# Squares of two norms added up on GpSimd and summed once by TensorE; the last norm's weights applied by feature and its turns moved ahead of the last products

## The chip, the cores and the metric

The kernel runs on one core of a Trainium2 chip. The core has TensorE (PE in the profile, with its weight loads as PEld), VectorE (DVE), ScalarE (ACT), GpSimd (POOL) and SyncE (SP), and 16 DMA engines that all queues share. The metric is the time of one execution on the device in microseconds; less is better.

## What is computed

One layer of a decoder, for a prompt of 512 tokens and for 8 sequences of 4 new tokens each (the sample group) that read a paged cache of keys and values. All is float32, the model is 1024 wide.

```python
h = _rmsnorm(x, norm1_w) * (1 + sc1) + sh1
z = h @ w_in                                  # 8 retention heads, 8 block-attention heads
...
x = x + g1 * (jnp.concatenate([ret_out, moba_out], axis=-1) @ w_out)
h2 = _rmsnorm(x, norm2_w) * (1 + sc2) + sh2   # the second norm
x = x + g2 * ((jax.nn.silu(h2 @ w_gate) * (h2 @ w_up)) @ w_down)
...
y_prompt = _rmsnorm(xp, final_w)              # the last norm
y_sample = _rmsnorm(xs, final_w)

def _rmsnorm(x, w):
    y = x * lax.rsqrt(jnp.mean(x * x, axis=-1, keepdims=True) + NORM_EPS)
    return y * w
```

## The kernel before

Everything is placed by hand: each engine has its own written-out order of instructions, and semaphores (`wait_ge`, `then_inc`) join them. No scheduler moves anything. Prompt activations lie turned, features on the 128 partitions and the 512 tokens along the row, so a tile `x2T[:, k, :]` (128x512) is feature tile k of eight (KT = 8). Products are made in three matmuls (`L1128` high part by high part, `L1129` low part of the activation, `L1130` low part of the weight).

Beside the prompt's work runs the sample group's attention over the cache, cut into 64 slots (page groups of 4 pages of 128 rows). In slot s, GpSimd has gathered the keys of the group into one of two buffers (`gather(g)`, L523, 1 MB, asynchronous; gather g waits until VectorE has turned group g - 2), VectorE turns them (L1846), TensorE multiplies them with the queries (`keys(s)`, L1161, at the slot's head), and 12 slots later TensorE weighs the values (`weigh`, L1216), whose pages SyncE loads as their buffers come free. At slots that are a multiple of 8, VectorE makes the block sums (L1859 to L1862) right behind the turn of the next group, and TensorE takes them (`block_gates`, L1180).

The output projection is slots 43 to 50 (`R_OUT` = 43, f = 0 to 7), one tile f of 24 matmuls in each. VectorE adds tile f to the residual (`residual`, L2126), and ScalarE squares it into one of two buffers (`stage[f % 2]`, L950). TensorE then sums each square over its features: `sum_squares(k)`, four 128x1 matmuls against ones (eight records in the trace, L1551), adding all eight tiles up in a PSUM bank. After the eighth, VectorE, ScalarE, TensorE and GpSimd turn the sums into 1/rms for each token, spread over all partitions in `rb`, and scale and split the tiles (slots 51 to 53) before the FFN's first product.

In GpSimd's order stand, beside the gathers, the rotation of the sample's queries and keys in iterations 46 and 47 (L532 to L535, products with `pool.drain()` between them; the next instruction does not start before the drain is done), two masked products in iteration 48 (L541), and the eight scalings of the norm in iterations 54 and 55 (L566).

The down projection, `R_DOWN`, is 24 steps d, 6 for each pair of feature tiles; steps 4 and 5 of a pair finish its two tiles, `evict_down` adds them to the residual. The last norm of the prompt comes after all of them: TensorE turns the eight feature tiles back into four token tiles of 128x1024 (32 turns of 128x128, L1722), ScalarE squares each with a running sum (L1058) and takes the root (L1060), VectorE inverts (L2332) and multiplies with 1/rms and with the weights `fw`, which lie along the row (L2334), and SyncE stores the tile (L512):

```python
for i in range(TT):
    final_norm(i)      # VectorE: wait for root i, reciprocal, scale by 1/rms and fw
```

The vectors that are needed by feature (norm weights among them) are loaded as rows at the start into `vrow`, by five small loads on ScalarE's queue, and turned by TensorE into `vT`, one column for each feature tile.

## Time and profile before

| | |
|---|---|
| median of 3 runs | 1039.37 us (1035.85 to 1046.96) |
| profiled execution, its own time | 1034.07 us |
| its span in the trace | 1032.2 us |
| mean granted clock of TensorE | 0.976 |
| busy: PE, DVE, ACT, POOL | 961.6, 624.5, 338.4, 139.4 us |
| DMA moved | 269.14 MB, 261 GB/s on the mean |

The span runs from the first to the last record; the profiled execution took 1.9 us more around it. Busy times are sums of records and say nothing of who waits for whom; the chain of waits does, from the last instruction back to the first.

### The profile page before, as it was taken

How to read it: one execution, taken by the hardware profiler on the slowest of the kernel's cores; microseconds unless marked ns; L12 is line 12 of the kernel's file. 1: busy time of each engine (PE TensorE's matmuls, PEld its weight loads, DVE VectorE, ACT ScalarE, POOL GpSimd, SP SyncE). 2: the span in 40 equal slices, each digit the busy share in tenths (PEclk: the TensorE clock that was granted, in tenths of full speed). 3: DMA queues.
4: the chain of work that ended last, by engine and by line, in shares of the span. 5: the costliest groups of instructions: out<-in, count | busy, mean ns of one | idle time of the engine just before them, and what ended most of it. 6: DMA issues, size and time to landing. Idle time of an engine off the chain costs nothing.

```text
span 1032.2 us, 20974 instructions
## 1 busy us (share of the span) xinstructions
PE 961.6 (93%) x7919; PEld 675.8 (65%) x7919; DVE 624.5 (60%) x1067; ACT 338.4 (33%) x735; POOL 139.4 (14%) x129
## 2 busy tenths in 40 slices
PE   3879998999999987979989999999999999999996
PEld 2557775766666644547756767676777777777775
DVE  1566874677767667876788584432655555453244
ACT  5412233334333624542252152332333222121113
POOL 0011111444210132204151220000000000000000
PEclk9899999999999989999989899999999999999998
DMA  9978877999786889988998668778476988787652
GB/s 340 364 257 282 284 252 268 296 274 300 255 287 215 276 320 390 356 288 280 362 320 285 231 230 265 230 228 267 144 218 167 240 226 231 218 251 248 204 194 87
DMA packets 217973, 269.14 MB, mean 261 GB/s; under 512 B 13473, under 2 KB 168425, under 8 KB 209682
## 3 DMA queue, kind: packets, MB, share of 16 engines
q1 hardware_dynamic: 110226, 126.65, 38.7%
q10 hardware_dynamic: 98432, 74.04, 23.6%
q0 software_dynamic: 9216, 67.11, 17.7%
q8 instruction: 63, 1.03, 0.4%
q14 instruction: 36, 0.29, 0.1%
HBM read 260.04 MB, written 5.64 MB: 257 GB/s over the span
## 4 chain that ended last, share of the span: by engine, by line
PE 72%; DVE 8%; DMA 7%; issue 5%; SPq 4%; DVEq 2%; ACT 1%; POOLq 1%; POOL 1%; ACTq 0%
PE banks L1128 13%; PE banks L1129 12%; PE banks L1130 12%; PE banks L1078 6%; PE banks L1216 4%; PE banks L1141 4%; PE banks L1143 4%; PE banks L1142 4%; PE banks L1161 4%; DVE KT L1846 3%; DMA V<-in_cache_v 3%; DMA K<-in_cache_k,kidx 1%; SPq L420 1%; PE banks L1340 1%; DMA early<-in_w_mod 1%
## 5 line engine op out<-in xcount | busy, mean ns | idle before, releaser
L658 ACT ACTIVATE whi<-raw 128x1024 fp32r<-128x1024 f32 (+1 forms) x76 | 78.6, 1035 | 298.0 <-PE banks L1130 144.4
L1128 PE MATMUL banks<-ahi,whi 128*128 128x512 f32 x416 | 169.2, 407 | 0.1
L1846 DVE STREAM_TRANSPOSE KT<-K 128x2048 f32<-128x2048 f32 x63 | 145.5, 2310 | 30.0 <-DMA K<-in_cache_k,kidx 15.1
L1129 PE MATMUL banks<-alo,whi 128*128 128x512 f32 x416 | 163.5, 393 | 0.0
L1130 PE MATMUL banks<-ahi,rawlo 128*128 128x512 f32 x416 | 163.3, 393 | 0.0
L1809 DVE TENSOR_TENSOR rawlo<-raw,whi 128x1024 fp32r<-128x1024 f32 (+1 forms) x76 | 91.3, 1201 | 54.3 <-ACT whi L658 51.2
L523 POOL DMA_INDIRECT K<-in_cache_k,kidx x64 | 64.0, 1000 | 412.4 <-DVE KT L1846 363.7
L1128 PEld LDWEIGHTS banks<-ahi,whi 128*128 128x128 f32 x416 | 78.7, 189 | 31.2 <-issue 13.1
L1141 PE MATMUL banks<-ahi,whi 128*128 128x512 f32 x216 | 90.2, 417 | 1.2 <-DVE rawlo L1816 0.9
L1130 PEld LDWEIGHTS banks<-ahi,rawlo 128*128 128x128 f32 x416 | 78.8, 189 | 17.3
L1161 PE MATMUL banks<-KT,qbd 128*32 128x128 f32 x2048 | 74.0, 283 | 15.7 <-DVE KT L1846 13.0
L1129 PEld LDWEIGHTS banks<-alo,whi 128*128 128x128 f32 x416 | 78.8, 189 | 14.9
L1143 PE MATMUL banks<-ahi,rawlo 128*128 128x512 f32 x216 | 85.1, 394 | 0.0
L1142 PE MATMUL banks<-alo,whi 128*128 128x512 f32 x216 | 84.9, 393 | 0.0
L1161 PEld LDWEIGHTS banks<-KT,qbd 128*32 128x32 f32 x2048 | 56.7, 112 | 29.7 <-issue 14.1
L1216 PE MATMUL banks<-V,pT 128*32 128x512 f32 x368 | 64.4, 630 | 11.5 <-DMA V<-in_cache_v 11.4
L1816 DVE TENSOR_TENSOR rawlo<-raw,whi 128x1024 fp32r<-128x1024 f32 x28 | 35.8, 1279 | 30.4 <-ACT whi L651 14.9
L1141 PEld LDWEIGHTS banks<-ahi,whi 128*128 128x128 f32 x216 | 40.9, 190 | 17.9 <-issue 7.5
L748 ACT ACTIVATE pm<-banks,st 128x128 f32<-128x128 f32 (+3 forms) x32 | 16.6, 524 | 96.8 <-DVE st L1989 91.4
L1143 PEld LDWEIGHTS banks<-ahi,rawlo 128*128 128x128 f32 x216 | 40.8, 189 | 9.4
L1142 PEld LDWEIGHTS banks<-alo,whi 128*128 128x128 f32 x216 | 41.1, 190 | 7.3
L1750 DVE TENSOR_TENSOR xtmp<-xtmp,banks 32x256 f32<-32x256 f32 x90 | 37.5, 417 | 7.1 <-issue 0.4
(330 smaller groups left out, 1462.1 us busy)
## 6 DMA issues: line engine op xcount, KB each, us to landing
V<-in_cache_v SPq DMA_DIRECT2D x184, 256.0 KB
rawm<-in_w_mod ACTq DMA_DIRECT2D x14, 1024.0 KB
raw<-in_w_in ACTq DMA_DIRECT2D x12, 1024.0 KB
zT<-in_cache_v SPq DMA_DIRECT2D x48, 256.0 KB
raw<-in_w_gate ACTq DMA_DIRECT2D x22, 512.0 KB
raw<-in_w_up ACTq DMA_DIRECT2D x22, 512.0 KB
srw<-in_w_gate SPq DMA_DIRECT2D x22, 512.0 KB, 5.6
srw<-in_w_up SPq DMA_DIRECT2D x22, 512.0 KB, 7.3
```

What stands on the lines that cost most here:

```text
L523: pool.indirect_dma_start(Kb[g % 2][:, :], None, ck, bass.IndirectOffsetOnAxis(kidx[:, g:g + 1], 0)).then_inc(s_k[g % 2], 16)
L658: act.activation(whi[t % 2][:, 0:kd, :], raw[u][:, 0:kd, t % 2 * P:(t % 2 + 1) * P], ACT.Copy).then_inc(s_hi, 1)
L1128: pe.matmul(out[:, :], whi[t % 2][:, k, :], hi(k), start=(first and n == 0), stop=False)
L1129: pe.matmul(out[:, :], whi[t % 2][:, k, :], lo(k), start=False, stop=False)
L1130: last = pe.matmul(out[:, :], low[:, k, :], hi(k), start=False, stop=(final and n == kd - 1))
L1141: pe.matmul(DB[:, :], whi[m % 2][:, k, :], ahi[:, k, :], start=(k == 0), stop=False)
L1142: pe.matmul(DB[:, :], whi[m % 2][:, k, :], alo[:, k, :], start=False, stop=False)
L1143: last = pe.matmul(DB[:, :], wlow[:, k, :], ahi[:, k, :], start=False, stop=(k == KT - 1))
L1161: last = pe.matmul(LG[32 * gq:32 * gq + 32, (g % 4) * P:(g % 4 + 1) * P], qbd[g // NGRP % 2][:, j, :], KTb[:, :, j, :], start=(jj == 0), s ...
L1216: pe.matmul(VO[32 * pg:32 * pg + 32, :], pT[:, n, 32 * pg:32 * pg + 32], bufs[pg][:, :], start=(n == 0), stop=(n == NGRP - 1)).then_inc(s_ ...
L1809: tt(rawlo[u][:, 0:kd, cols], raw[u][:, 0:kd, cols], whi[t % 2][:, 0:kd, :].bitcast(F32), ALU.subtract).then_inc(s_lo, 1)
L1846: dve.transpose(KTb[:, :, :, :], Kb[g % 2][:, :]).then_inc(s_kt, 1)
```

## The change

For the second norm, ScalarE squares feature tile 0 into `rb`, and tiles 1 to 6 into the two stage buffers as before. GpSimd adds tile k (1 to 6) into `rb` in iteration 47 + k of its loop (`add_squares`), between a gather and the next, and drains before it counts up `s_sqa`. ScalarE waits for that count instead of TensorE's before it uses a stage buffer again. TensorE makes two groups of sums, one of `rb` and one of tile 7, both after the last tile.

For the last norm the same is done in buffers `x3q(k)`: ScalarE squares each tile after its eviction, GpSimd adds tiles 1 to 6 into tile 0, and TensorE sums twice. VectorE multiplies each evicted tile by its weights (`vT`, eight more columns, from a sixth small load on ScalarE's queue) into `x3w(k)`, and TensorE turns these instead of `x2T`: 18 turns (three token tiles, features 0 to 5) go ahead of the last two product tiles, the other 14 stay behind. One inverse and one root serve all four token tiles; ScalarE scales tiles 0 and 2 out of PSUM and VectorE tiles 1 and 3. The sample group's last norm is as it was.

```diff
--- before.py
+++ after.py
@@ -40,8 +40,8 @@
 NMOD, NMA = 24, 8
-V_BMOD, V_N1, V_N2, V_GN, V_MN = 0, 48, 56, 64, 68
-NVEC = 72
+V_BMOD, V_N1, V_N2, V_GN, V_MN, V_FW = 0, 48, 56, 64, 68, 72
+NVEC = 80
@@ -276,6 +276,10 @@
     fw = at(A, "fw", [P, DM])
     ytok = [at(A + 1024 + DM * i, f"ytok{i}", [P, DM]) for i in range(TT)]
+    x3q = lambda k: ytok[k // 2][:, k % 2 * T:(k % 2 + 1) * T]
+    xwb = at(A + 1024 + DM * TT, "xwb", [P, KT - 2, T])
+    x3w = lambda k: xwb[:, k, :] if k < KT - 2 else stage[k - KT + 2]
     two_banks = [persist.enter_context(nc.psum_tensor(f"banks{i}", [P, 2, 512], F32)) for i in range(4)]
     bank01 = two_banks[0]
     bank = [two_banks[i // 2][:, i % 2, :] for i in range(8)]
@@ -352,7 +356,7 @@
+    s_nx, s_gmt, s_sqa = sem("x2_scaled"), sem("gmod_turned"), sem("x2_squares_added")
...
+    X3Q, X3A, X3W, X3S, X3I, X3R = KT, KT - 2, KT, 2, RSPREAD, 1
     kview = lambda w: w[0].rearrange("(k p) f -> p k f", p=P)
     w_mod_v, w_in_v, w_out_v = kview(w_mod), kview(w_in), kview(w_out)
@@ -508,7 +516,7 @@
         sp.wait_ge(s_y, 1)
         sp.dma_start(y_sample.rearrange("b t d -> (b t) d"), x2s[:, :]).then_inc(s_out, 16)
         for i in range(TT):
-            sp.wait_ge(s_y, i + 2)
+            sp.wait_ge((s_yr, s_y)[i % 2], i // 2 + 2)
             sp.dma_start(y_prompt[0, i * P:(i + 1) * P, :], ytok[i][:, :]).then_inc(s_out, 16)
         sp.wait_ge(s_kss, 48)
         sp.wait_ge(s_kst, 64)
@@ -565,10 +573,20 @@
                 pool.wait_ge(s_r1, RSPREAD)
             pool.tensor_tensor(zT[:, k, :], zT[:, k, :], rb[:, :], ALU.mult).then_inc(s_nx, 1)
+        def add_squares(k):
+            pool.wait_ge(s_sqx, k + 1)
+            pool.tensor_tensor(rb[:, :], rb[:, :], stage[k % 2][:, :], ALU.add)
+            pool.drain().then_inc(s_sqa, 1)
         def scale_heads(hp):
             pool.wait_ge(s_hrs, hp + 2)
             o = rettok[:, hp, :].rearrange("p (c d) -> p c d", d=HD)
             pool.tensor_tensor(o, o, gain[:, hp, 0:8].unsqueeze(2).broadcast_to((P, H, HD)), ALU.mult).then_inc(s_hn, 1)
+        def add_x3_squares(k):
+            pool.wait_ge(s_sqx, X3Q + k + 1)
+            pool.tensor_tensor(x3q(0), x3q(0), x3q(k), ALU.add)
+            pool.drain().then_inc(s_sqa, 1)
         pool.wait_ge(s_idx, 1)
         pool.wait_ge(s_hi, 1)
@@ -589,6 +607,8 @@
                 pool.wait_ge(s_hrs, 1)
                 heads = mobatok.rearrange("p i (h d) -> p i h d", h=H)
                 pool.tensor_tensor(heads, heads, gain[:, 4:8, 0:8].unsqueeze(3).broadcast_to((P, TT, H, HD)), ALU.mult).then_inc(s_hm, 1)
+            if 1 <= g - R_OUT - 4 < KT - 1:
+                add_squares(g - R_OUT - 4)
             if g in (R_NORM + 3, R_NORM + 4):
                 for k in range(4):
                     scale_x(4 * (g - R_NORM - 3) + k)
@@ -614,12 +634,16 @@
                 masked_k(b)
                 masked_k(b + 1)
+        for k in range(1, KT - 1):
+            add_x3_squares(k)
     @block.scalar
     def _(act):
         act.dma_start(vrow[V_BMOD:V_N1, :], b_mod[0].rearrange("(r c) -> r c", c=P)).then_inc(s_vec, 16)
         for a, v in ((V_N1, norm1_w), (V_N2, norm2_w), (V_GN, ret_gn_w), (V_MN, moba_norm_w)):
             n = v.shape[1] // P
             act.dma_start(vrow[a:a + n, :], v[0].rearrange("(r c) -> r c", c=P)).then_inc(s_vec, 16)
+        act.dma_start(vrow[V_FW:NVEC, :], final_w.rearrange("(r c) -> r c", c=P)).then_inc(s_vec, 16)
         act.dma_start(xs[:, :], x_sample.rearrange("b t d -> (b t) d")).then_inc(s_xs, 16)
         act.wait_ge(s_c, 32)
         act.activation(crow[:, :], crow[:, :], ACT.Silu).then_inc(s_silu, 1)
@@ -945,9 +969,9 @@
                 split_out(f + 1)
             if f >= 1:
                 act.wait_ge(s_ev, F_OUT + f + 2)
-                if f >= 3:
-                    act.wait_ge(s_ssm, f - 2)
-                act.activation(stage[(f - 1) % 2][:, :], x2T[:, f - 1, :], ACT.Square).then_inc(s_sqx, 1)
+                if f >= 4:
+                    act.wait_ge(s_sqa, f - 3)
+                act.activation(rb[:, :] if f == 1 else stage[(f - 1) % 2][:, :], x2T[:, f - 1, :], ACT.Square).then_inc(s_sqx, 1)
             if f == KT - 1:
                 exps(B_NORM)
             if f:
@@ -957,7 +981,7 @@
         act.activation(st2[:, 28:29], C("eps"), ACT.Sqrt)
         act.wait_ge(s_ev, F_OUT + KT + 2)
-        act.wait_ge(s_ssm, KT - 2)
+        act.wait_ge(s_sqa, KT - 3)
         act.activation(stage[1][:, :], x2T[:, KT - 1, :], ACT.Square).then_inc(s_sqx, 1)
         slot(R_NORM)
         next_chunk(5)
@@ -1043,6 +1067,10 @@
                 keep_gate(m // 2)
             sample_slot(s)
             slot(s)
+        def x3_squares(k):
+            act.wait_ge(s_ev, F_DOWN + k + 1 + 2)
+            act.activation(x3q(k), x2T[:, k, :], ACT.Square).then_inc(s_sqx, 1)
         for d in range(6 * DM // CHUNK):
             t = KT + 2 * FT + d
             if d % 2 == 0:
@@ -1052,12 +1080,19 @@
             if d == 0:
                 keep_hidden(FT - 1)
             sample_slot(R_DOWN + d)
-        for i in range(TT):
-            act.wait_ge(s_yt, i + 1)
-            act.activation(ytok[i][:, :].rearrange("p (e c) -> p e c", e=2), TURNED[i][:, :, :], ACT.Square, accum_out=st[:, 16 + i:17 + i])
-            act.drain()
-            act.activation(st2[:, 16 + i:17 + i], st[:, 16 + i:17 + i], ACT.Sqrt, scale=1.0 / DM, bias=C("eps")).then_inc(s_yr, 1)
+            fb, e = divmod(d - 5, 6)
+            if fb >= 0 and e < 2:
+                x3_squares(2 * fb + e)
+        x3_squares(KT - 1)
+        act.wait_ge(s_r1, X3I + 1)
+        act.activation(st2[:, 24:28], st2[:, 16:20], ACT.Sqrt).then_inc(s_r2, 1)
+        act.drain()
+        for i in (0, 2):
+            act.wait_ge(s_yt, 1)
+            act.activation(ytok[i][:, :].rearrange("p (e c) -> p e c", e=2), TURNED[i][:, :, :], ACT.Copy,
+                           scale=st2[:, 24 + i:25 + i]).then_inc(s_yr, 1)
     @block.tensor
     def _(pe):
@@ -1067,7 +1102,7 @@
         for k in range(KT):
             last = pe.transpose(bank[4][:, k * NSEQ:(k + 1) * NSEQ], crow[:, k * P:(k + 1) * P], ident[0:NSEQ, 0:NSEQ])
         last.then_inc(s_ctp, 1)
-        pe.wait_ge(s_vec, 80)
+        pe.wait_ge(s_vec, 96)
         pe.transpose(bank[5][:, 0:NVEC], vrow[:, :], ident[0:NVEC, 0:NVEC]).then_inc(s_vtp, 1)
         pe.wait_ge(s_ct, 1)
@@ -1543,14 +1578,18 @@
-        def sum_squares(k):
-            if k == 0:
-                pe.matmul(DB[:, 0:TT], ident, C("pad0")[:, 0:TT], start=True, stop=False, skip_group_check=True)
-            pe.wait_ge(s_sqx, k + 1)
+        def sum_over_features(out, src, final):
             for i in range(TT):
-                last = pe.matmul(DB[:, i:i + 1], stage[k % 2][:, i * P:(i + 1) * P], ones[:, 0:1], start=False, stop=(k == KT - 1),
-                                 skip_group_check=True)
-            last.then_inc(s_ssm, 1)
+                last = pe.matmul(out[:, i:i + 1], src[:, i * P:(i + 1) * P], ones[:, 0:1], start=False, stop=final, skip_group_check=True)
+            return last
+        def sum_squares():
+            pe.matmul(DB[:, 0:TT], ident, C("pad0")[:, 0:TT], start=True, stop=False, skip_group_check=True)
+            pe.wait_ge(s_sqa, KT - 2)
+            sum_over_features(DB, rb, False)
+            pe.wait_ge(s_sqx, KT)
+            sum_over_features(DB, stage[1], True).then_inc(s_ssm, 1)
         for f in range(KT):
             slot_head(R_OUT + f)
@@ -1564,11 +1603,9 @@
                  last_in=(lambda: turn_heads(3)) if f == 0 else None)
             if f == KT - 1:
                 slot_head(R_NORM)
-            if f:
-                sum_squares(f - 1)
             if f == KT - 1:
                 turn_probs(B_NORM, 0)
-                sum_squares(KT - 1)
+                sum_squares()
             slot_rest(R_OUT + f)
@@ -1704,6 +1741,9 @@
             sample_slot(s)
             slot_rest(s)
+        def turn_x3(i, k):
+            return pe.transpose(TURNED[i][:, k // 4, (k % 4) * P:(k % 4 + 1) * P], x3w(k)[:, i * P:(i + 1) * P], ident)
         for d in range(6 * DM // CHUNK):
             fb, n, half = d // 6, d // 2 % 3, d % 2
             pe.wait_ge(s_fl, 8 * n + KD[n] + 1)
@@ -1712,15 +1752,33 @@
             tile(KT + 2 * FT + d, bank[2 * (fb % 2) + half], lambda k: unit(8 * n + k)[:, 0], lambda k: unit(8 * n + k)[:, 1],
                  KD[n], first=(n == 0), final=(n == 2))
             sample_slot(R_DOWN + d)
-        for i in range(TT):
-            for k in range(KT):
-                if i == 0 and k == 0:
-                    pe.wait_ge(s_ev, F_DOWN + 7 + 2)
-                if i == 0 and k == KT - 1:
-                    pe.wait_ge(s_ev, F_DOWN + 8 + 2)
-                last = pe.transpose(TURNED[i][:, k // 4, (k % 4) * P:(k % 4 + 1) * P], x2T[:, k, i * P:(i + 1) * P], ident)
-            last.then_inc(s_yt, 1)
+            if d == 6 * DM // CHUNK - 3:
+                pe.wait_ge(s_x3, 1)
+                pe.wait_ge(s_nx, X3W + KT - 2)
+                for i in range(TT - 1):
+                    for k in range(KT - 2):
+                        turn_x3(i, k)
+        pe.wait_ge(s_nx, X3W + KT - 1)
+        for i in range(TT - 1):
+            turn_x3(i, KT - 2)
+        for k in range(4):
+            turn_x3(TT - 1, k)
+        pe.wait_ge(s_nx, X3W + KT)
+        for i in range(TT - 1):
+            last = turn_x3(i, KT - 1)
+        last.then_inc(s_yt, 1)
+        sums = TURNED[TT - 1][:, 1, :]
+        pe.matmul(sums[:, 0:TT], ident, C("pad0")[:, 0:TT], start=True, stop=False, skip_group_check=True)
+        pe.wait_ge(s_sqa, X3A + KT - 2)
+        sum_over_features(sums, x3q(0), False)
+        pe.wait_ge(s_sqx, X3Q + KT)
+        sum_over_features(sums, x3q(KT - 1), True).then_inc(s_ssm, 1)
+        pe.wait_ge(s_r1, X3I + 1)
+        for k in range(4, KT):
+            last = turn_x3(TT - 1, k)
+        last.then_inc(s_yt, 1)
     @block.vector
     def _(dve):
@@ -2156,7 +2214,7 @@
         residual(KT - 1, 16 + KT - 1, bank[(KT - 1) % 2])
         gained(KT - 1)
         turn_half_keys(R_NORM + 1, 0)
-        dve.wait_ge(s_ssm, KT)
+        dve.wait_ge(s_ssm, 1)
         then(ts(st2[:, 8:12], DB[:, 0:TT], 1.0 / DM, EPS, ALU.mult, ALU.add))
         dve.reciprocal(st2[:, 8:12], st2[:, 8:12]).then_inc(s_r1, 1)
         dve.wait_ge(s_r2, 1)
@@ -2164,7 +2222,7 @@
             last = ts(stage[0][:, i * P:(i + 1) * P], ident, st2[:, i:i + 1], None, ALU.mult)
         last.then_inc(s_r1, 1)
         turn_half_keys(R_NORM + 1, 1)
-        dve.wait_ge(s_ssm, KT + 1)
+        dve.wait_ge(s_ssm, 2)
         cp(rb[:, :], DB[:, :]).then_inc(s_r1, 1)
         slot_head(R_NORM + 1)
         slot_rest(R_NORM + 1)
@@ -2326,14 +2384,6 @@
             dve.scalar_tensor_tensor(x2s[:, :], x2s[:, :], st2[0:S, 1:2], fw[0:S, :], ALU.mult, ALU.mult)
             dve.drain().then_inc(s_y, 1)
-        def final_norm(i):
-            dve.wait_ge(s_yr, i + 2)
-            then(dve.reciprocal(st2[:, 16 + i:17 + i], st2[:, 16 + i:17 + i]))
-            by_half = lambda x: x.rearrange("p (e c) -> p e c", e=2)
-            dve.scalar_tensor_tensor(by_half(ytok[i][:, :]), TURNED[i][:, :, :], st2[:, 16 + i:17 + i], by_half(fw[:, :]), ALU.mult, ALU.mult)
-            dve.drain().then_inc(s_y, 1)
         o2 = sm[0:32, 0:512].rearrange("p (b d) -> p b d", b=NB_SEQ)
         def hidden_product(n):
@@ -2361,6 +2411,9 @@
         def evict_down(fb, half):
             dve.wait_ge(s_ft, F_DOWN + 6 * fb + 4 + half + 3)
             residual(2 * fb + half, 40 + 2 * fb + half, bank[2 * (fb % 2) + half])
+            k = 2 * fb + half
+            dve.drain()
+            ts(x3w(k)[:, :], x2T[:, k, :], vT[:, V_FW + k:V_FW + k + 1], None, ALU.mult).then_inc(s_nx, 1)
         for d in range(6 * DM // CHUNK):
             s = R_DOWN + d
@@ -2377,8 +2430,14 @@
                 evict_down(fb, e)
         evict_down(3, 1)
-        for i in range(TT):
-            final_norm(i)
+        dve.wait_ge(s_ssm, X3S + 1)
+        then(ts(st2[:, 16:20], TURNED[TT - 1][:, 1, 0:TT], 1.0 / DM, EPS, ALU.mult, ALU.add))
+        dve.reciprocal(st2[:, 16:20], st2[:, 16:20]).then_inc(s_r1, 1)
+        dve.wait_ge(s_r2, X3R + 1)
+        for i in (1, 3):
+            dve.wait_ge(s_yt, 1 + i // 2)
+            ts(ytok[i][:, :].rearrange("p (e c) -> p e c", e=2), TURNED[i][:, :, :], st2[:, 24 + i:25 + i], None, ALU.mult).then_inc(s_y, 1)
     persist.close()
```

GpSimd's order in iterations 48 to 53 and up to the norm's scalings, before. `K` are the two gather buffers, `kmask` the masked products, `rb` holds the norm's factors.

```order
L523 DMA K_61<-in_cache_k,kidx 128x2048
L541 TENSOR_TENSOR kmask_119<-krs,cts 32x512
L541 TENSOR_TENSOR kmask_120<-krs,cts 32x512
L523 DMA K_62<-in_cache_k,kidx 128x2048
L523 DMA K_61<-in_cache_k,kidx 128x2048
L523 DMA K_62<-in_cache_k,kidx 128x2048
L523 DMA K_61<-in_cache_k,kidx 128x2048
L523 DMA K_62<-in_cache_k,kidx 128x2048
L523 DMA K_61<-in_cache_k,kidx 128x2048
L566 TENSOR_TENSOR zT<-zT,rb 128x512 x4
```

And in the changed kernel, the first four iterations of it:

```order
L531 DMA K_61<-in_cache_k,kidx 128x2048
L578 TENSOR_TENSOR rb<-rb,stage_55 128x512
L549 TENSOR_TENSOR kmask_119<-krs,cts 32x512
L549 TENSOR_TENSOR kmask_120<-krs,cts 32x512
L531 DMA K_62<-in_cache_k,kidx 128x2048
L578 TENSOR_TENSOR rb<-rb,stage_54 128x512
L531 DMA K_61<-in_cache_k,kidx 128x2048
L578 TENSOR_TENSOR rb<-rb,stage_55 128x512
```

Each gather of iterations 48 to 53 now has an add (and its drain) between it and the next one; in iteration 48 the add stands ahead of the masked products.

TensorE's order at the very end, before (`ffb` are the FFN's hidden tiles, the last product tile ends with them; `ct` holds the identity and the ones):

```order
L1128 MATMUL banks<-ffb,whi_86 128x512
L1129 MATMUL banks<-ffb,whi_86 128x512
L1130 MATMUL banks<-ffb,rawlo_83 128x512
L1722 MATMUL banks<-ct,x2T 128x128 x32
L2383 UNCONDITIONAL_BRANCH
```

And in the changed kernel (the 18 earlier turns stand two product tiles ahead of these rows):

```order
L1165 MATMUL banks<-ffb,rawlo_83 128x512
L1745 MATMUL banks<-ct,stage_54 128x128 x3
L1745 MATMUL banks<-ct,xwb 128x128 x4
L1745 MATMUL banks<-ct,stage_55 128x128 x3
L1772 MATMUL banks<-ct 128x4
L1583 MATMUL banks<-ct,ytok_137 128x1 x4
L1583 MATMUL banks<-ct,ytok_140 128x1 x4
L1745 MATMUL banks<-ct,xwb 128x128 x2
L1745 MATMUL banks<-ct,stage_54 128x128
L1745 MATMUL banks<-ct,stage_55 128x128
```

Of the 32 turns behind the last product, 14 are left there, and a padding product and two groups of sums have come in between them.

## Rows read from the trace of the kernel before

**Rows 1.** The page, chain of waits by engine, share of the span

```profile
PE 72%; DVE 8%; DMA 7%; issue 5%; SPq 4%; DVEq 2%; ACT 1%; POOLq 1%; POOL 1%; ACTq 0%
```

**Rows 2.** Chain of waits, 440 to 560 us: start us, us, what

```profile
477.67 7.83 issue
...
489.52 6.85 DMA K<-in_cache_k,kidx
...
498.85 1.08 PE banks L1161 x32
...
526.63 0.79 PE banks L1551 x8
...
536.90 6.31 DMA zT<-in_cache_v
```

**Rows 3.** Timeline of GpSimd: start us, us, instruction, idle time before it

```profile
260.98 0.97 POOL L523 DMA_INDIRECT K<-in_cache_k,kidx  x1 [4.08 <-DVE KT L1846]
...
266.61 1.27 POOL L551 TENSOR_TENSOR zT<-zT,swapped 128x512 f32<-128x512 f32 x1 [1.78 <-issue]
...
475.05 1.16 POOL L523 DMA_INDIRECT K<-in_cache_k,kidx  x1 [0.78 <-issue]
...
485.53 0.73 POOL L535 TENSOR_TENSOR krs<-kmask,kmask 32x256 f32<-32x256 f32 x1 [7.86 <-issue]
...
490.51 2.05 POOL L541 TENSOR_TENSOR kmask<-krs,cts 32x512 f32<-32x512 f32 x2
...
531.40 4.96 POOL L566 TENSOR_TENSOR zT<-zT,rb 128x512 f32<-128x512 f32 x4
```

**Rows 4.** Timeline of VectorE in slots 46 to 50

```profile
485.38 2.31 DVE L1846 STREAM_TRANSPOSE KT<-K 128x2048 f32<-128x2048 f32 x1 [1.02 <-DMA K<-in_cache_k,kidx]
...
501.21 2.30 DVE L1846 STREAM_TRANSPOSE KT<-K 128x2048 f32<-128x2048 f32 x1
...
505.81 0.17 DVE L1862 TENSOR_TENSOR sm<-sm,ct 128x16 f32<-128x16 f32 x1
...
512.78 0.49 DVE L2131 TENSOR_SCALAR zT<-x2T,gain 128x512 f32<-128x512 f32 x1
...
520.91 2.30 DVE L1846 STREAM_TRANSPOSE KT<-K 128x2048 f32<-128x2048 f32 x1
```

**Rows 5.** Timeline of TensorE, block gates in slot 48

```profile
508.09 0.39 PE L1180 MATMUL banks<-sm,ct 128*128 128x16 f32 x2
```

**Rows 6.** Timeline of ScalarE, the second norm's root

```profile
527.90 0.20 ACT L965 ACTIVATE st<-st 128x4 f32<-128x4 f32 x1 [1.82 <-DVE st L2161]
```

**Rows 7.** Windows: busy by engine, then PEclk, DMA share, GB/s

```profile
532.00:533.00 1.00, 0.10 (x1) 0.00 (x0) 0.84 (x2) 0.29 (x1) 1.00 (x2) 1.00 1.14 389
...
534.00:535.00 1.00, 0.50 (x1) 0.14 (x2) 1.00 (x1) 1.00 (x4) 1.00 (x1) 0.92 0.99 395
```

**Rows 8.** Timeline of all engines, end of the program

```profile
1019.74 3.96 PE L1722 MATMUL banks<-ct,x2T 128*128 128x128 f32 x32
1019.94 0.75 DVE L2126 SCALAR_TENSOR_TENSOR x2T<-banks,mT,x2T 128x512 f32<-128x512 f32 x1 [3.33 <-PE banks L1130]
...
1021.11 1.03 ACT L1058 ACTIVATE ytok<-banks 128x1024 f32<-128x1024 f32 x1 [8.41 <-PE banks L1722]
...
1024.20 5.25 SPq L512 DMA_DIRECT2D out<-ytok  x4
...
1027.77 1.28 DVE L2334 SCALAR_TENSOR_TENSOR ytok<-banks,st,fw 128x1024 f32<-128x1024 f32 x1
```

**Rows 9.** DMA issues: engine, count, KB each, median us to landing

```profile
out<-ytok SPq DMA_DIRECT2D x4, 512.0 KB, 2.7
```

**Rows 10.** Windows of 1 us during the stores, columns as in rows 7

```profile
1030.00:1031.00 1.00, 0.00 (x0) 0.00 (x0) 0.00 (x0) 0.00 (x0) 0.00 (x0) 0.50 1.02 410
```

**Rows 11.** Timeline of ScalarE's queue at the start

```profile
1.18 0.92 ACTq L622 DMA_DIRECT2D vrow<-in_norm_w  x2
```

**Rows 12.** Chain of waits, 0 to 40 us

```profile
20.90 12.53 DMA early<-in_w_mod
```

1 line of the change is left out of this document (removed).

## The prediction

> **What bounds the kernel now.** I read the chain of waits first, since a busy share says nothing of what is late. It is 72% TensorE [rows 1], so anything taken off TensorE looks like gain. The second thing to read is therefore where that chain leaves TensorE near the two norms. In the output projection (slots 43 to 50) it does: it passes through idle time on GpSimd of 7.83 us, then through the gather of key page group 48, issued at 489.52 and landed 6.85 us later, its turn on VectorE, and only at 498.85 back to TensorE [rows 2]. GpSimd sits idle there in a drain. It issued gather 47 at 475.05, had two short products to do, and the next instruction behind its drain starts at 485.53 [rows 3]; VectorE, which waited for that very page group, starts turning it at 485.38 [rows 4]. So a drain on GpSimd lets go when the gather issued ahead of it has landed, 0.15 us apart. The same at gather 260.98: the instruction behind the drain starts at 266.61, 5.6 us after [rows 3]. From 498.85 to the end of the norm's sums at 527.42 (526.63 + 0.79) the chain stays on TensorE, then goes to the value pages that SyncE loads as buffers come free, the last landing at 543.21 [rows 2]. At the end of the program the chain is the last residual, the turns, ScalarE's squares, four scalings on VectorE and the stores [rows 8].
>
> **The second norm's sums.** Eight groups of small matmuls become two. One group is worth 0.79 us on the chain [rows 2]. Groups 0 to 3 lie ahead of 498.85, where TensorE takes up what the gather of 48 gave: its 4 x 0.79 = 3.2 us become waiting, gain 0. Groups 4 and 5 lie behind it, at most 1.6 us.
>
> **What is added there.** Six adds of 128x512 on GpSimd, in iterations 48 to 53 of its loop, each right behind the gather of that iteration and each with a drain. The add itself is 4.96 / 4 = 1.24 us [rows 3] and would be hidden. The drain is not: as read above it holds GpSimd until the gather has landed, so gather g+1, the semaphore for the sums, and the two masked products of iteration 48 (2.05 us [rows 3]) are queued behind it. Where two gathers could be in flight, there is one. A gather's time until the drain lets go is 5.6 us at its best [rows 3], 6.85 us for number 48 [rows 2] and 10.5 us for 47 [rows 3], which shared the transfer engines with more. I take 6.2, between the first two, because the stage is the same as that of 48 but with fewer transfers at once.
>
> Step by step. Gather 48 is fixed by GpSimd and lands at 496.4. Behind it the masked products end at 498.5, so gather 49 is issued at 498.6 and lands at 504.8 or a little later, say 505.2 with the value pages beside it. VectorE turned page group 49 at 501.21 and had the block sums of that iteration ready at 505.98, 4.8 us later [rows 4]; now 510.0. TensorE took them at 508.09 [rows 5], so it is late by 1.9 us. Of this it wins back 0.8 (group 5), but VectorE's turn of group 50 is late too, and 1.5 us remain. The turn of group 51 ended at 523.2 (520.91 + 2.30) [rows 4], now at 524.7. Gather 53 waits for that turn and, by the row of gathers, for 52: issue 525.0, landed 531.2. Only then has the sixth add its semaphore, on which TensorE's two groups wait, 1.6 us: they end at 532.8 where they ended at 527.42. That is **+5.4 us**. Bounds: with 5.6 us for a gather and no delay ahead, 523.3 + 5.6 + 1.6 = 530.5, +3.1. With 8 us each, the gathers 49 to 53 in a row end at 498.6 + 40 + 0.8 = 539.4, and the sums at 541.0, +13.6.
>
> Who waits for it: TensorE's weighings of slots 50 and 51 stand behind the sums in its order, the loads of the next value pages wait for those weighings, and FFN's first tile waits for these pages [rows 2]. The norm's own chain (inverse, root, spread, eight products on GpSimd, the split) moves with it. So the whole is passed on. ScalarE's squares now wait for the adds instead of TensorE: that of feature tile 3 can start when gather 48 has landed, 496.5, and it and the copy of the scores behind it, two short instructions, have 2.3 us until TensorE wants that copy at 498.85 [rows 2]; nothing.
>
> **The clock.** TensorE has nothing to do from 527 to 531 now. In the trace it stopped early in the row of 532, and the granted clock began to fall from 2.4 to 1.2 GHz in the row of 534 [rows 7]. If it falls in the new wait, the two sums and the two weighings behind (1.6 + 1.8 us) run at half speed: 0 to +3.4, I take the middle, **+1.6 us**.
>
> **The last norm.** Of its 32 turns, 18 go ahead of the last two product tiles. TensorE has no gap there, so they are not hidden but push the end of the products: 18 x 3.96 / 32 = 2.2 us [rows 8], from 1019.9 to 1022.1. Each eviction gets a drain and a product by weight, 0.49 us [rows 4], of which only the last is on the path; seven lie in VectorE's idle time. From there: residual 0.75 [rows 8], drain and weight 0.6, to 1023.5; three turns 0.4; padding and two groups 1.8, to 1025.7; inverse and root 0.68 as from 527.42 to 528.10 [rows 2, 6]; one scaling on ScalarE 1.03 [rows 8], so that the first store can be issued at 1027.5. VectorE makes two of the four tiles from 1026.4 on, at 1.28 each at most [rows 8]: the fourth is ready at 1029.0, as before. The adds on GpSimd have no gather left ahead, and their drains cost nothing there.
>
> What is late next are the stores. They were issued from 1024.20 on over 5.25 us [rows 8], each landed in 2.7 us [rows 9]. The most that a microsecond moved was 410 GB/s [rows 10]: four of 512 KB are 2.1 MB, 5.1 us, and 1.3 of the 2.7 us are one store's own bytes. Now: 1027.5 + 1.4 + 5.1 + 0.4 to the span's end = 1034.4 against 1032.2, **+2.2 us**. Bounds: if the fourth tile's readiness set the end, 0; if from the first issue on it takes the 8.0 us that it took before (1032.2 - 1024.2), +3.3.
>
> **The start.** One more small load ahead of xs on ScalarE's queue, 0.46 us [rows 11]. The chain there is in the loads of w_mod until 33.4 [rows 12], which cover it: 0, at most 0.5 without them.
>
> **A rule.** The gathers above took 5.6 to 10.5 us. The Trainium skill, page "DMA: Bandwidth & Descriptors", section "Anatomy of one DMA — SWDGE (gpsimd) path", fits 2.0 us plus bytes over 436 GB/s, an estimate of 4.4 us for 1 MB, by which the sums would be late by 2 us only; every gather in the rows took longer, and I stay with the rows.
>
> **Sum.** 5.4 + 1.6 + 2.2 = +9.2 us on the profiled execution: 1034.07 to 1043.3 us. The median of the runs stands 5.3 us above that execution, so I forecast 1048.5.
>
> **Rivals.** (a) *The drain waits only for GpSimd's own work.* Then the six adds are hidden, 1.6 us are saved, and the tail remains: 1.6 off, 2.2 on, +0.6, 1040.0 on the median. Against it stand the two drains read above. (b) *Gathers in a row take 8 us each*, as 47 did or worse, because 1 MB of value pages and half a MB of weights go along in every slot. 13.6 + 1.6 + 2.2 = +17.4, about 1057. (c) *TensorE is the bound after all*: the gathers come early enough, so that all six groups (6 x 0.79 = 4.7 us) are won and the stores are not late. The profiled 1034.07 becomes 1029.4 and the median 1034.7, 4.7 us faster. It decides from a gather that lets the drain go within some 3 us; nothing in the trace is that short, and 1% faster would need twice the saving.
>
> **Chances.** Forecast 0.60; (b) 0.17; (a) 0.15; (c) 0.08. About 1% (10.4 us) is what a measurement of this kernel can tell from no change. The forecast's own range is +5 to +13, of which a third is above 10.4: with (b), slower 0.37. Faster by over 1% is a remnant of (c), 0.05. The rest, 0.58, is within 1%. The range takes in (a) but for its lowest part, and (b) up to its price: 1038 to 1058.
>
> **What would show it.** In the profile after, GpSimd's next gather starts 5.6 to 8 us behind the one before in iterations 48 to 53, TensorE is idle ahead of the line that sums rb, and its sums end near 533 instead of 527. Near the end there is a block of 18 turns between product tiles, the first store is issued near 1027.5 + 7 us of shift, and the stores overlap at around 400 GB/s. If the gathers stay as close as before, (a) is right, and the whole of the +5.4 falls. If the sums come early but the end is late, the tail alone is the cause. The most likely error is the size of the gather's time, since five of them add up.

## The result and the profile after

| | before | after |
|---|---|---|
| median | 1041.23 us (1035.85 to 1046.96, 4 runs) | 1060.26 us (1054.73 to 1063.79, 4 runs) |
| ratio | 1 | 1.0184, 95% interval 1.0138 to 1.023 |
| profiled execution | 1034.07 us, span 1032.2 | 1057.73 us, span 1055.1 |
| gather 48's issue to the end of the second norm's sums | 37.9 us | 52.9 us |
| last product's end to the span's end | 12.3 us | 12.6 us, and 2.1 for 18 turns ahead |

The change makes the kernel 1.8% slower, some 19 us. Against the page before [rows 1], the chain of waits has less of TensorE and more of GpSimd's queue and of waiting without a releaser:

```profile
PE 69%; DVE 9%; DMA 7%; issue 7%; SPq 2%; DVEq 2%; POOLq 2%; ACT 1%; POOL 1%; ACTq 0%
```

A warning on comparing two profiled executions comes first. Gather 48 was issued at 489.52 before and at 493.97 after, 4.45 us later. At 170 us nothing is late yet (a gather at 169.03 before stands at 168.14 after). A kernel below that has no edit at all ahead of gather 48 (e4) issues it at 492.78, and one without an edit ahead of gather 46 (e9) issues that at 469.13 instead of 463.85. Kernel e1, with only the small load and the vectors' turn edited ahead of it, issues gather 48 at 498.36, 8.8 us late, and yet its runs are 0.13% over the kernel before. The profiled execution before was itself a short one, 1034.07 us against a median of 1041.23. So 5 to 9 us come and go between executions of nearly the same instructions, and I count every time below from the issue of gather 48 of the same execution. Counted like this, of the 22.9 us by which the span grew 4.45 lie ahead of gather 48, 15.0 between it and the end of the sums, and 3.5 behind.

The timeline of GpSimd in the stage of [rows 3], after (start us, us, instruction, idle time before it):

```profile
493.97 0.97 POOL L531 DMA_INDIRECT K<-in_cache_k,kidx  x1 [0.80 <-issue]
494.97 1.30 POOL L578 TENSOR_TENSOR rb<-rb,stage 128x512 f32<-128x512 f32 x1
502.15 2.03 POOL L549 TENSOR_TENSOR kmask<-krs,cts 32x512 f32<-32x512 f32 x2 [5.88 <-issue]
504.34 0.98 POOL L531 DMA_INDIRECT K<-in_cache_k,kidx  x1 [0.16 <-DVE KT L1904]
...
512.15 0.95 POOL L531 DMA_INDIRECT K<-in_cache_k,kidx  x1 [5.54 <-issue]
...
518.66 0.95 POOL L531 DMA_INDIRECT K<-in_cache_k,kidx  x1 [4.25 <-issue]
...
527.96 0.95 POOL L531 DMA_INDIRECT K<-in_cache_k,kidx  x1 [7.03 <-issue]
...
536.08 0.95 POOL L531 DMA_INDIRECT K<-in_cache_k,kidx  x1 [5.86 <-issue]
```

L531 is the gather, L578 the new add, L549 the masked products. The add ends at 496.3, and GpSimd starts nothing until 502.15: that is the drain, and in the chain the same gather lands at 493.97 + 7.98 = 501.95. Gather 49 then waits for the two masked products, and each one from 50 on starts behind a drain. The DMA issues of the profile have the time to landing for two more, in windows around the issues of gathers 50 and 52:

```profile
K<-in_cache_k,kidx POOLq DMA_INDIRECT x1, 5.7
K<-in_cache_k,kidx POOLq DMA_INDIRECT x1, 7.3
```

They land at 517.9 and 535.3, and the next gathers, 51 and 53, start 0.8 us later. From the first gather to the last are 42.1 us (34.0 before), where VectorE's turns used to set the pace.

What waits for that, in the timelines of ScalarE and TensorE after:

```profile
502.12 0.63 ACT L974 ACTIVATE stage<-x2T 128x512 f32<-128x512 f32 x1 [9.22 <-POOLq L579]
...
504.43 1.93 PE L1196 MATMUL banks<-KT,qbd 128*32 128x128 f32 x32 [4.45 <-DVE KT L1904]
...
543.29 1.86 PE L1583 MATMUL banks<-ct,rb 128*128 128x1 f32 x8 [6.39 <-POOLq L579]
545.01 1.84 PE L1583 MATMUL banks<-ct,stage 128*128 128x1 f32 x8
546.79 1.93 PE L1251 MATMUL banks<-V,pT 128*32 128x512 f32 x8
```

TensorE has keys late, here by 4.45 us, and stands still for 6.39 us ahead of the sums, released by the queue entry of line 579, the drain. A group of sums takes 1.8 us where one took 0.79 [rows 2]. The window shows TensorE's granted clock (busy by engine, then PEclk, DMA share, GB/s): it is at its lower level, 1.2 GHz, from 542 to 551 us.

```profile
542.00:551.00 9.00, 7.71 (x33) 4.58 (x34) 2.37 (x7) 0.87 (x5) 0.95 (x1) 0.50 0.31 86
```

The end of the program, against [rows 8 to 10], in the timeline, in the DMA issues and in a window of 1 us during the stores, one fence each:

```profile
1044.40 1.93 PE L1583 MATMUL banks<-ct,ytok 128*128 128x1 f32 x16
...
1047.05 2.48 DVE L2440 TENSOR_SCALAR ytok<-banks,st 128x1024 f32<-128x1024 f32 x2 [0.27 <-ACT st L1089]
1047.10 2.12 ACT L1093 ACTIVATE ytok<-banks,st 128x1024 f32<-128x1024 f32 x2
...
1048.24 2.80 SPq L520 DMA_DIRECT2D out<-ytok  x4
```

```profile
out<-ytok SPq DMA_DIRECT2D x4, 512.0 KB, 3.8
```

```profile
1050.00:1051.00 1.00, 0.00 (x0) 0.00 (x0) 0.00 (x0) 0.00 (x0) 0.00 (x0) 0.50 1.04 426
```

The four stores are issued within 2.8 us instead of 5.25, but each lands after 3.8 us instead of 2.7, and the bytes go out at 385 to 430 GB/s in each microsecond from 1049 to 1054: from there on the stores set the end.

### The profile page after: what moved, and what is told of

It is laid out like the page before. It is cut to its first block, busy times and chain, and to the rows that moved or that the text cites. A ratio compares the mean times of both kernels' runs of the same rounds, so it can differ in the third digit from the quotient of the medians.

```text
span 1055.1 us, 20941 instructions
## 1 busy us (share of the span) xinstructions
PE 968.0 (92%) x7889; PEld 677.2 (64%) x7889; DVE 631.5 (60%) x1071; ACT 339.7 (32%) x734; POOL 155.6 (15%) x141
## 3 DMA queue, kind: packets, MB, share of 16 engines
q0 software_dynamic: 9216, 67.11, 17.2%
## 4 chain that ended last, share of the span: by engine, by line
PE 69%; DVE 9%; DMA 7%; issue 7%; SPq 2%; DVEq 2%; POOLq 2%; ACT 1%; POOL 1%; ACTq 0%
PE banks L1163 12%; PE banks L1164 11%; PE banks L1165 11%; PE banks L1113 6%; PE banks L1176 4%; PE banks L1251 4%; PE banks L1177 4%; PE banks L1178 4%; DVE KT L1904 4%; PE banks L1196 3%; DMA V<-in_cache_v 3%; DMA K<-in_cache_k,kidx 2%; DMA rawm<-in_w_mod 2%; PE banks L1375 1%; DVEq L1796 1%
## 5 line engine op out<-in xcount | busy, mean ns | idle before, releaser
L1904 DVE STREAM_TRANSPOSE KT<-K 128x2048 f32<-128x2048 f32 x63 | 145.5, 2310 | 38.8 <-DMA K<-in_cache_k,kidx 25.8
L531 POOL DMA_INDIRECT K<-in_cache_k,kidx x64 | 64.0, 999 | 415.9 <-DVE KT L1904 340.3
L1196 PEld LDWEIGHTS banks<-KT,qbd 128*32 128x32 f32 x2048 | 55.8, 112 | 37.1 <-issue 20.0
L1251 PE MATMUL banks<-V,pT 128*32 128x512 f32 x368 | 63.6, 644 | 14.2 <-DMA V<-in_cache_v 13.4
```

The costliest lines, as they stand in the source:

```text
L531: pool.indirect_dma_start(Kb[g % 2][:, :], None, ck, bass.IndirectOffsetOnAxis(kidx[:, g:g + 1], 0)).then_inc(s_k[g % 2], 16)
L1196: last = pe.matmul(LG[32 * gq:32 * gq + 32, (g % 4) * P:(g % 4 + 1) * P], qbd[g // NGRP % 2][:, j, :], KTb[:, :, j, :], start=(jj == 0), s ...
L1251: pe.matmul(VO[32 * pg:32 * pg + 32, :], pT[:, n, 32 * pg:32 * pg + 32], bufs[pg][:, :], start=(n == 0), stop=(n == NGRP - 1)).then_inc(s_ ...
L1904: dve.transpose(KTb[:, :, :, :], Kb[g % 2][:, :]).then_inc(s_kt, 1)
```

## The experiments

Each time is a ratio to the kernel before, run on the same chip, with its 95% interval. The two stage times are from one profiled execution each: from the issue of gather 48 to that of gather 53, and to the end of the second norm's sums.

| kernel | ratio | to gather 53 | to the sums' end |
|---|---|---|---|
| before | 1 | 34.0 us | 37.9 us |
| after | 1.0184 (1.0138 to 1.023) | 42.1 | 52.9 |
| e1_tail_only | 1.0013 (0.9992 to 1.0035) | 33.2 | 37.1 |
| e2_norm_only | 1.0153 (1.0116 to 1.019) | 43.7 | 55.1 |
| e3_self_wait | 1.0074 (1.0045 to 1.0102) | 35.6 | 39.9 |
| e4_drains_only | 1.0043 (1.0014 to 1.0072) | 39.6 | 43.6 |
| e5_adds_first | 1.0037 (1.0014 to 1.0061) | 35.4 | 38.8 |
| e6_adds_first_old_end | 1.0021 (0.9992 to 1.005) | 37.3 | 40.6 |
| e7_sem_at_add | 1.0091 (1.0053 to 1.0129) | 39.3 | 43.7 |
| e8_filler | 1.0117 (1.0071 to 1.0163) | 41.2 | 49.8 |

**The two norms apart.** The first kernel is the changed one with the old sums put back, the second the old one with the new sums alone.

In e1, against the changed kernel (ScalarE's waits go back to TensorE's semaphore too):

```diff
-            if 1 <= g - R_OUT - 4 < KT - 1:
-                add_squares(g - R_OUT - 4)
...
+            if f:
+                sum_squares(f - 1)
             if f == KT - 1:
                 turn_probs(B_NORM, 0)
-                sum_squares()
+                sum_squares(KT - 1)
```

In e2, against the kernel before, the same lines with + and - the other way round.

Expected of e1:

> The changed kernel with the second norm as it was before (eight groups of sums on TensorE, no adds on GpSimd); the last norm, its adds, its 18 early turns, the extra small load and the stores stay changed. My theory (second norm costs some 15 us, tail 2 to 3 us): the span is 2 to 3 us over the kernel before, time 1.000 to 1.005 of it; gathers 48 to 53 come as before and the sums of the second norm end near 527 us. It also tells whether the 4.5 us by which the changed kernel was late at gather 48, with no edit ahead of it but the small load, come from that load: then this one has them too and is at 1.005 to 1.009. Rival (the tail is what costs, the second norm is free): ratio 1.015 to 1.02.

Expected of e2:

> The kernel before with the second norm of the changed one (six adds with drains on GpSimd, two groups of sums) and nothing else. My theory: 13 to 17 us slower, ratio 1.012 to 1.017; gathers 48 to 53 stand 6.5 to 9 us apart, each issued just after a drain lets go, and the sums end 14 to 16 us later than before, TensorE at 1.2 GHz in them. Rival (tail is what costs): ratio under 1.004.

The second norm costs 1.53%, 16 us; all of the last norm, with its extra load at the start, 0.13%, 1.3 us with an interval from -0.8 to 3.6. The two add up to 1.0166, inside the interval of the whole. The rival, that the end of the program costs, is out. The small load is not what made gather 48 late in the changed kernel: e1 has it and is at 1.0013, not at 1.005 to 1.009. In the stage e2 shows the changed kernel's pattern, with gathers up to 11.0 us apart and sums 17.2 us later than before, both somewhat more than I expected. The last drain and the sums in its chain of waits (start us, us, what):

```profile
540.18 8.04 POOLq L571
548.26 3.57 PE banks L1555 x16
```

The 18 early turns stand in the chain of e1, between product tiles, with their price:

```profile
1018.56 1.97 PE banks L1743 x18
```

**The drain or the adds.** The same six adds at the same places, but each gives its semaphore itself, and the next waits for that.

```diff
+            if k > 1:
+                pool.wait_ge(s_sqa, k - 1)
-            pool.tensor_tensor(rb[:, :], rb[:, :], stage[k % 2][:, :], ALU.add)
-            pool.drain().then_inc(s_sqa, 1)
+            pool.tensor_tensor(rb[:, :], rb[:, :], stage[k % 2][:, :], ALU.add).then_inc(s_sqa, 1)
```

> The changed kernel with the six adds of the second norm kept on GpSimd, at the same place behind each gather, but without a drain: each add gives its semaphore itself, and the next one waits for that semaphore. Theory (the drain waits for the gather's landing, so that one gather is in flight where two were): two gathers are in flight again, the sums end within 2 us of 527 (from 2 us earlier to 2 later, against 19 us later with drains), the time is 12 to 16 us under the changed kernel and 1 to 4 over the kernel before, ratio 1.000 to 1.005. Rival 1 (the adds themselves cost: GpSimd's and VectorE's access to memory slow each other, instructions of VectorE such as 1.48 and 1.89 us where 0.49 was usual): ratio stays at 1.012 or more. Rival 2 (a semaphore from an add is given only when the gather ahead has landed, too): gathers 6.5 us or more apart as with drains, ratio 1.015 to 1.02.

The timeline of GpSimd in e3:

```profile
494.15 0.97 POOL L531 DMA_INDIRECT K<-in_cache_k,kidx  x1 [0.80 <-issue]
495.15 1.30 POOL L580 TENSOR_TENSOR rb<-rb,stage 128x512 f32<-128x512 f32 x1
496.40 3.22 POOL L549 TENSOR_TENSOR kmask<-krs,cts 32x512 f32<-32x512 f32 x2
499.78 0.98 POOL L531 DMA_INDIRECT K<-in_cache_k,kidx  x1 [0.16 <-issue]
```

Gather 49 follows 48 by 5.6 us, not 10.4: two are in flight again, and 13.0 of the stage's 15.0 us are gone. So the drain is most of the cost, and an add's own semaphore does not wait for the gather. The time misses what I expected: 1.0074, outside 1.000 to 1.005, with an interval that only touches it. The stage shows +2.0 us and e1 has +1.3; some 4 us of the 7.7 have no row that I can name. The profiled execution of e3, 1041.95 us, is also the fastest of its twelve (median 1048.82), so its rows may not hold what the other runs lost.

The adds do have a smaller price of their own. Beside an add, VectorE's scaling of 128x512 by the gain takes 1.48 us in e3 and in the changed kernel alike, where 0.49 is usual [rows 4]. The Trainium skill, page "GPSIMD Engine Reference", section "1. Specifications", says that GpSimd shares its SBUF interfaces with VectorE and that instructions of VectorE with two inputs from SBUF or in a 2-port mode contend there. The trace agrees that they contend, 1.48 against 0.49; which of the two this one is, no run here shows. In the timelines of VectorE and GpSimd in e5 it looks like a hold for the whole of the add: an instruction on 128x8, which takes 0.23 us elsewhere, starts beside one and ends 0.03 us after it.

```profile
522.54 1.35 DVE L1961 TENSOR_SCALAR sm<-sm 128x8 f32<-128x8 f32 x1
522.56 1.30 POOL L580 TENSOR_TENSOR rb<-rb,stage 128x512 f32<-128x512 f32 x1 [0.90 <-ACT stage L977]
```

**The drain alone.** In the kernel before:

```diff
+            if R_OUT + 5 <= g < R_OUT + 11:
+                pool.drain()
```

> The kernel before with six bare drains on GpSimd, one behind each of the gathers 48 to 53, no adds; all sums stay on TensorE. Theory (the drain is the cost): the gathers stand 6 to 9 us apart as in the changed kernel, but TensorE's sums need no semaphore from GpSimd, so that only the late key pages cost: 5 to 12 us slower, ratio 1.005 to 1.012. Rival (the adds cost, a drain with nothing of GpSimd's own to wait for is free): ratio 0.998 to 1.002, gathers as close as before.

```profile
492.78 0.97 POOL L523 DMA_INDIRECT K<-in_cache_k,kidx  x1 [0.80 <-issue]
499.26 2.03 POOL L541 TENSOR_TENSOR kmask<-krs,cts 32x512 f32<-32x512 f32 x2 [5.50 <-issue]
501.45 0.97 POOL L523 DMA_INDIRECT K<-in_cache_k,kidx  x1 [0.16 <-DVE KT L1848]
509.82 0.94 POOL L523 DMA_INDIRECT K<-in_cache_k,kidx  x1 [7.40 <-issue]
```

With no work of GpSimd's to wait for, a bare drain holds it for 5.5 us, until the gather has landed (the chain has 6.30 us for it, to 499.08). The cost is 5.7 us in the stage, of the changed kernel's 15.0, and 0.43% in the runs, 4.5 us, a little under what I expected. This is the cost of the drains with what follows from the late gathers, TensorE's lower clock behind its waits among it (below). The rest needs someone who waits for the drain's semaphore.

**The semaphore apart from the drain.** All six drains stay, but the count is given by the add:

```diff
-            pool.tensor_tensor(rb[:, :], rb[:, :], stage[k % 2][:, :], ALU.add)
-            pool.drain().then_inc(s_sqa, 1)
+            pool.tensor_tensor(rb[:, :], rb[:, :], stage[k % 2][:, :], ALU.add).then_inc(s_sqa, 1)
+            pool.drain()
```

> The changed kernel with its six drains kept where they are, but the semaphore for ScalarE and TensorE given by the add and not by the drain behind it. It parts the two costs of the drain: gathers one at a time, and sums that wait for the landing of gather 53. If bare drains cost 5.7 us in the profile and the rest of the 15 us is the wait for the last landing and TensorE's low clock in it, the gathers stay 6 to 9 us apart, the sums start within 1 us after the sixth add, at full clock, and end 44 to 48 us after gather 48's issue (52.9 in the changed kernel): 5 to 9 us faster than the changed kernel, ratio 1.009 to 1.014 of the kernel before. Rival (a semaphore given at the add waits for the drained gather too, or the waits of other engines set the time): sums 51 to 53 us after gather 48, ratio 1.016 or more.

The chain of waits in e7, at the fifth and the sixth add:

```profile
535.41 1.21 POOLq L579
536.65 1.28 POOL rb L578
...
537.97 1.95 PE banks L1583 x16
539.92 3.52 PE banks L1251 x16
```

The sums start as the sixth add ends, and 9.2 us of the stage are gone, a little more than I expected; the time is 0.9% over the kernel before, half of what was lost. This shows the second cost: TensorE and ScalarE waiting for landings that they have no use for. TensorE still has 1.8 us of idle time there, and its clock falls a little later: both groups of sums take 1.95 us together, but the two weighings behind 3.52.

**The clock.** The changed kernel, with work for TensorE in the wait (the products' result is overwritten):

```diff
         def sum_squares():
+            for _ in range(7):
+                pe.matmul(DB[:, :], ident, x2T[:, 0, :], start=True, stop=True, skip_group_check=True)
```

> The changed kernel with seven products of the identity by 128x512 of x2T on TensorE, into a bank that nothing uses yet, in the wait ahead of the second norm's sums; their result is overwritten. It measures the clock's part alone. Theory (the granted clock falls to 1.2 GHz because TensorE is idle in the 6.4 us wait, and the work behind it runs at half speed for some 8 us): the clock stays at 2.4 GHz from the wait to the weighings, the two groups of sums take 1.6 us (3.7 in the changed kernel), the two weighings 1.9 (3.9), and the time is 3 to 5 us under the changed kernel, ratio 1.013 to 1.016. Rival (the clock is not on the path, because value pages or VectorE are late behind it anyway): same time as the changed kernel, 1.018, though the clock is high.

Its chain of waits, and then its window over the sums (PEclk is the last column but two):

```profile
541.08 6.01 PE banks L1588 x14
547.21 1.78 PE banks L1583 x16
548.99 1.85 PE banks L1251 x16
```

```profile
545.00:549.00 4.00, 4.00 (x27) 2.82 (x29) 0.00 (x0) 0.00 (x0) 0.00 (x0) 1.00 0.91 285
```

Busy in the wait, TensorE keeps 2.4 GHz; sums and weighings take 3.6 us together, not 7.1. The stage ends 3.1 us earlier, of which 0.9 are the gathers' (41.2 against 42.1). The ratio, 1.0117, is below the range that I gave, and its interval (1.0071 to 1.0163) overlaps that of the changed kernel (1.0138 to 1.023). So the runs point to a gain but do not give its size; the 3.5 us are from the rows of one profile each.

This fills only the last wait. From 490 to 530 us, ahead of it, the clock (the last column but two) differs too. The windows of the kernel before, the changed one, e1 and e4, in this order:

```profile
490.00:530.00 40.00, 39.75 (x385) 29.63 (x380) 30.29 (x48) 13.24 (x36) 7.28 (x8) 1.00 0.92 327
490.00:530.00 40.00, 32.51 (x281) 22.88 (x280) 30.20 (x45) 7.13 (x9) 15.96 (x16) 0.88 0.83 280
490.00:530.00 40.00, 39.86 (x378) 30.87 (x375) 31.29 (x51) 10.12 (x21) 10.74 (x11) 1.00 0.90 320
490.00:530.00 40.00, 35.98 (x318) 27.38 (x317) 25.22 (x47) 8.69 (x16) 8.70 (x10) 0.91 0.77 266
```

In the changed kernel TensorE runs at 1.2 GHz from 504 to 510 us, behind its wait of 4.45 us for keys, and again from 528 to 530. In e3 to e8 the same comes behind TensorE's first longer wait of the stage, for 3 to 7 us. What these stretches cost is part of each stage time above; no run here takes them out.

**Is there a gain to be had from the adds?** Gather 53 waits for VectorE, and the sixth add stands behind it. In these two kernels there are no drains, and the adds 3 to 6 stand ahead of their gathers; e5 has the new end, e6 the old one.

```diff
         for g in range(2, NG):
+            if R_OUT + 7 <= g < R_OUT + 11:
+                add_squares(g - R_OUT - 4)
             pool.wait_ge(s_kt, g - 1)
             gather(g)
-            if 1 <= g - R_OUT - 4 < KT - 1:
+            if g in (R_OUT + 5, R_OUT + 6):
                 add_squares(g - R_OUT - 4)
```

> The changed kernel with its adds without drains (each waits for the semaphore of the one before) and the adds 3 to 6 put ahead of the gathers 50 to 53, where GpSimd waited for VectorE anyway. My theory (what was left of the loss without drains is that the sixth add stands behind gather 53, which waits for VectorE): TensorE does not wait for the sums; from gather 48's issue to the end of the sums 36 to 38 us (37.9 before, 39.9 with adds behind the gathers and no drains, 52.9 in the changed kernel), clock full in the sums. Time: the old sums with the new end were at 1.0013, so 0.998 to 1.003 of the kernel before. Rival (adds on GpSimd slow VectorE down, whatever their place): 1.005 or more.

> The kernel before, its last norm untouched, with the second norm of the run before this one: adds on GpSimd without drains, 3 to 6 ahead of their gathers, two groups of sums on TensorE. Theory (at most 1.6 us of sums lie on the path and are now won): 0.5 to 1.6 us faster, ratio 0.997 to 1.000. Rival (gathers and VectorE, not TensorE, set this stage, nothing is won): 0.999 to 1.002. Slower than 1.004 would speak for a cost of the adds themselves.

In e5 TensorE does not wait for the sums, and yet they end 38.8 us after gather 48, 0.9 later than before and outside my 36 to 38; in e6 they end at 40.6. The ratios, 1.0037 (1.0014 to 1.0061) and 1.0021 (0.9992 to 1.005), are both above what I expected: neither kernel is faster than the one before, and e5 is slower, clear of noise. The chain of waits of e5 tells a part of where the six groups' 4.7 us went:

```profile
515.76 0.75 DVE x2T L2187
...
517.01 1.22 DVE rawlo L1870
518.23 2.23 DVE KT L1907
520.50 1.08 PE banks L1199 x32
```

The stage runs over VectorE: a residual, a split of weights, the turn of a page group, and only then TensorE's keys. What TensorE saves on the group behind its block gates it spends waiting for that turn. The groups ahead of the keys of slot 48 become part of its wait for them, 4.07 us in e5, and the clock behind that wait is at 1.2 GHz from 503 to 506 us in e5 and from 509 to 515 in e6. In e5 TensorE needs 10.0 us from there to the end of its block gates, with a group less, where it needed 9.6 before. So the adds showed no gain here, with or without a drain. How much of that is VectorE's order, how much the clock, and how much the adds' hold on VectorE, no run parts.

**The same drain elsewhere.** [rows 2 and 3] show the kernel before stalled for 7.83 us in a drain of the sample's rotation. If drains are what costs, taking those out should help.

```diff
-            pool.drain()
+            pool.wait_ge(s_rh, done + 2)
             pool.tensor_tensor(o[:, :, half, :], ta, tb, op).then_inc(s_rh, 1)
-            pool.drain()
+            pool.wait_ge(s_rh, done + 3)
```

> The kernel before, its two norms untouched, with the drains of the sample's rotations on GpSimd (iterations 46 and 47) taken out: the products give a semaphore and the instruction behind waits for it. The theory carried to another place: a drain there holds gather 48 until 47 has landed. Then gather 48 is issued when VectorE has turned page group 46, 5 to 8 us earlier than the 14.5 us behind gather 47 that it took before, and 2 to 7 us of that reach the end: ratio 0.993 to 0.998. Rival (value pages and VectorE set this stage anyway, the chain's way through the drain was a near tie): 0.999 to 1.002, although gather 48 comes earlier.

> The run before this one, with the drains of the eight rotations of retention's queries and keys on GpSimd (iterations from 168 us to 270 us) replaced in the same way too. In the profile before those drains are short (1.0 to 1.8 us where a gather was outstanding, 0.2 us elsewhere), since each rotation waits for its swapped copy while the gather lands. Theory: nothing more than the run before it, within 0.002. Rival (those short drains are on the path too): a further 2 to 5 us, 0.002 to 0.005 lower.

> The run before this one with the second norm's adds on GpSimd, without drains, 3 to 6 ahead of their gathers, and two groups of sums on TensorE. If gathers come early enough that TensorE sets the stage, its six groups of 0.79 us count: up to 4.7 us less than the run before it, 0.002 to 0.005 lower. If VectorE's turns and gates set it, as the chain of the run with adds first showed: within 0.002 of the run before it.

The ratios are 1.0002 (0.9973 to 1.0032), 0.9999 (0.9972 to 1.0027) and 1.0033 (1.001 to 1.0056). The stall is gone, and nothing is won: I had forecast 0.993 to 0.998 for e9, and its rival came true, with e10 no different from it. The timeline of GpSimd in e9, then a window of 22 us, then the chain of waits:

```profile
476.66 0.97 POOL L523 DMA_INDIRECT K<-in_cache_k,kidx  x1 [0.90 <-DVE KT L1847]
483.97 0.97 POOL L523 DMA_INDIRECT K<-in_cache_k,kidx  x1 [0.81 <-DVE KT L1847]
```

```profile
484.00:506.00 22.00, 22.00 (x245) 17.03 (x244) 11.76 (x20) 4.14 (x6) 4.91 (x5) 1.00 1.05 375
```

```profile
493.81 11.89 DMA raw<-in_w_out
505.72 1.07 ACT whi L659
```

Gather 48 goes out 7.3 us behind 47 instead of 14.5. For the 22 us that follow, the transfer engines are busy throughout (share 1.05) at 375 GB/s, and the last weights of the output projection, 1 MB, need 11.89 us, so that ScalarE and then TensorE wait for them. From gather 46 to the end of the sums e9 takes 63.2 us, the kernel before 63.6. The stall in the drain was covered by a bound that stands right behind it. The adds of e11 bring nothing either: it is slower than e10 by more than the 0.002 that I expected at most, and with e5 the second kernel with adds and no drains whose interval lies above 1. No kernel tried beats the one before.

## Why the prediction was wrong

I forecast 1048.5 us, +9.2 on the profiled execution, in a range up to 1058; it came out at 1060.26, with the sign of the forecast and twice its size. What happened is the rival of gathers in a row at 8 us each, priced at about 1057, to which I had given 0.17.

- **The reading of the bound held.** The drain waits for the gather's landing: shown by e3 (without it most of the cost goes) and e4 (a bare drain has it). Rivals (a), a drain that waits only for GpSimd's own work, and (c), TensorE as the bound, are out.
- **The step that failed is the size of a gather's time in "I take 6.2, between the first two".** It measured 7.98 us for gather 48, 5.7 and 7.3 for 50 and 52, and from a gather's issue to the next instruction behind its drain 6.5 to 9.3 us, 7.9 on the mean of the six; the 0.8 us from a landing to the next gather's issue was not in the forecast at all. I had put gather 53's issue 35.5 us behind that of 48, its landing 6.2 later and two groups of 1.6, to 43.3 us. Measured: 42.1, then 7.2, then 3.6, to 52.9. Of the 9.6 us that were missing, 6.6 lie in the gathers ahead, 1.0 in the last one and 2.0 in the clock, which I had in a term of its own. My value lay between two single gathers, 5.6 and 6.85, and the third, the 10.5 of 47 just ahead of this stage, I had set aside. With 6.2 us, VectorE's turn (524.7) came later than the row of gathers (498.6 + 4 x 6.2 = 523.4) and set gather 53's issue; with 7.9 the row sets it, and every gather's excess counts.
- **"Who waits": ScalarE's squares, put down as nothing, waited 9.22 us.** Behind that square stand the copy of scores and a split of weights. Gather 53 stood at 39.6 and 39.3 us where nobody waited for the drain's semaphore (e4, e7), and at 41.2, 42.1 and 43.7 where ScalarE did (e8, after, e2). That fits a loop of late squares, late copies and late turns worth 2 to 4 us, but with one profile each it is argued and not shown.
- **The clock, +1.6 us in a range of 0 to 3.4**, was at the upper end: 3.5 us in the sums and weighings by e8's rows. The forecast looked at the last wait alone; the clock was low in two more stretches of the stage, 504 to 510 and 528 to 530 us, whose price is open.
- **The gain was put at 1.6 us at most.** It is nothing: in e5, where TensorE waits for no sums, the stage is not shorter. The chain before stays on TensorE from 498.85 to 527.42 [rows 2], but the chain of e5, with two groups less on TensorE there, leads over VectorE.
- **The last norm, +2.2 us**, holds: 2.1 us for the turns and 0.3 behind the last product in the rows after, stores as the bound at 385 to 430 GB/s, and 1.3 us (-0.8 to 3.6) in the runs of e1. **The start, 0**, holds: e1 has that load too.
